# Feed-forward layers of a two-layer decoder step: eight block products per weight panel become seven

## What is computed

```python
def sq_relu_mlp(xn, w_up, w_down):
    h = jax.nn.relu(xn @ w_up)          # (tokens, 1024) @ (1024, 4096)
    return (h * h) @ w_down             # (tokens, 4096) @ (4096, 1024)

h = h + sq_relu_mlp(rmsnorm(h, g_mlp[l]), w_up[l], w_down[l])
```

## Time and profile before

| | |
|---|---|
| median of three runs | 1596.13 us |
| profiled execution, first to last instruction | 1593.0 us |
| feed-forward of layer 0 (32 panels) | about 378 to 788 us |
| feed-forward of layer 1 (32 panels) | about 1164 to 1587 us |
| busy share of TensorE / VectorE / ScalarE / GpSimd | 99 / 44 / 41 / 27 % |
| granted TensorE clock, mean | 0.999 |

### The profile page before, as it was taken

How to read it: one execution, slowest core, us unless ns; L and a number is a source line. 1 busy time by engine, 2 the same in 40 slices (tenths; PEclk the granted TensorE clock), 3 DMA queues, 4 the chain that set the end, 5 groups by cost and what they waited for, 6 DMA issues and landing times.

```text
span 1593.0 us, 34954 instructions
## 1 busy us (share of the span) xinstructions
PE 1575.9 (99%) x13744; PEld 1503.1 (94%) x13744; DVE 694.3 (44%) x1349; ACT 652.3 (41%) x996; POOL 434.9 (27%) x382
## 2 busy tenths in 40 slices
PE   8999999999999999999999999999999999999998
PEld 8999999989999999999998888887999999999998
DVE  8866666663212112112335888889532121121223
ACT  6544444433313213223334777678433132231333
POOL 3000000003443333434342211111433334344331
PEclk9999999999999999999999999999999999999999
DMA  6233332222222322222235554554222222222221
GB/s 190 54 100 83 82 82 84 91 88 80 81 82 77 106 79 79 79 79 79 79 97 190 203 178 146 160 174 134 72 65 92 91 79 80 79 79 79 79 80 60
DMA packets 169516, 158.11 MB, mean 99 GB/s; under 512 B 5388, under 2 KB 160084, under 8 KB 169428
## 3 DMA queue, kind: packets, MB, share of 16 engines
q1 hardware_dynamic: 151346, 147.34, 29.2%
q10 hardware_dynamic: 18082, 9.48, 2.1%
HBM read 145.00 MB, written 11.80 MB: 98 GB/s over the span
## 4 chain that ended last, share of the span: by engine, by line
PE 97%; DVE 1%; issue 1%; ACT 0%; DMA 0%; DVEq 0%; ACTq 0%
PE acc L2012 70%; PE acc L2359 6%; PE pM L2417 3%; PE acc L2272 1%; PE pL L2132 1%; PE pO L2431 1%; PE pL L2400 1%; PE acc L2474 1%; PE pO L2463 1%; PE acc L2491 1%; PE pM L2201 1%; PE acc L2463 1%; PE acc L2656 1%; PE pL L2183 1%; PE pL L2155 0%
## 5 line engine op out<-in xcount | busy, mean ns | idle before, releaser
L490 POOL TENSOR_TENSOR wlo<-wraw,whi 128x512 fp32r<-128x512 f32 x288 | 365.7, 1302 | 904.8 <-ACT whi L583 904.8
L2012 PE MATMUL acc<-xa_hi,whi 128*128 128x288 f32 x1568 | 344.4, 301 | 0.0
L2012 PE MATMUL acc<-xa_hi,wlo 128*128 128x288 f32 x1568 | 335.8, 296 | 0.0
L2012 PE MATMUL acc<-xa_lo,whi 128*128 128x288 f32 x1568 | 335.3, 295 | 0.0
L583 ACT ACTIVATE whi<-wraw 128x2048 fp32r<-128x2048 f32 x90 | 172.0, 1911 | 305.6 <-PE acc L2012 300.7
L2012 PE MATMUL acc<-xb_hi,whi 128*128 128x288 f32 x1200 | 257.9, 297 | 0.8 <-issue 0.8
L2012 PEld LDWEIGHTS acc<-xa_hi,whi 128*128 128x128 f32 x1568 | 250.8, 189 | 7.2 <-issue 4.6
L2012 PE MATMUL acc<-xb_hi,wlo 128*128 128x288 f32 x1200 | 257.0, 296 | 0.0
L2012 PE MATMUL acc<-xb_lo,whi 128*128 128x288 f32 x1200 | 256.9, 296 | 0.0
L2012 PEld LDWEIGHTS acc<-xa_hi,wlo 128*128 128x128 f32 x1568 | 252.3, 188 | 0.0
L2012 PEld LDWEIGHTS acc<-xa_lo,whi 128*128 128x128 f32 x1568 | 251.9, 188 | 0.0
(11 more groups left out here) (427 smaller groups left out, 2094.5 us busy)
## 6 DMA issues: line engine op xcount, KB each, us to landing
wraw<-in_w_up_dram SPq DMA_DIRECT2D x64, 512.0 KB, 4.6
wraw<-in_w_down_dram SPq DMA_DIRECT2D x64, 512.0 KB, 4.0
Kp<-in_cache_k_dram SPq DMA_DIRECT2D x32, 512.0 KB, 4.2
Vp<-in_cache_v_dram SPq DMA_DIRECT2D x32, 512.0 KB, 5.3
wraw<-in_w_in_a_dram SPq DMA_DIRECT2D x30, 512.0 KB, 5.6
wraw<-in_w_kv_dram SPq DMA_DIRECT2D x16, 512.0 KB, 4.3
St<-in_state_hgrn_dram ACTq DMA_DIRECT2D x8, 512.0 KB, 6.3
out_dram<-Sn ACTq DMA_DIRECT2D x8, 512.0 KB, 4.8
```

The source lines that it names most:

```text
L490: ins = pool.tensor_tensor(wlo[s][:, k:k + 2, :], wraw[s][:, k:k + 2, :], whi[s][:, k:k + 2, :].bitcast(F32), ALU.subtract)
L2012: last = pe.matmul(acc[a][:, hf, 0:HALF], w[s][:, k, a * P:(a + 1) * P], x[:, k, hf * HALF:(hf + 1) * HALF], start=(k == 0 and n == 0), st ...
```

## The change

Both feed-forwards are computed by Strassen's scheme, in Winograd's form. A panel is seen as a 2x2 matrix of blocks: even or odd k in depth, first or second output block of 128. The activations are seen as 2x2 as well: even or odd k, first or second token half. Instead of 8 block products there are 7, each of depth 4 x 128 into one PSUM bank. The kernel calls such a panel a quad and numbers them by `G`; r = G mod 8 is its place in a chunk, 0 to 3 up and 4 to 7 down. A quad is 7 x 4 x 3 = 84 matmuls. The last chunk's down projection of layer 1 stays as it was (`last_down`), so 60 of 64 panels change.

- Weights: VectorE makes four sums and differences of 512 columns a quad (`sum1` to `sum4`). The seven pieces are each split into high part by ScalarE (`piece_high`) and low part by GpSimd (`piece_low`), 512 columns each. There is one set of seven piece buffers for high and one for low; a piece is replaced when its product of the quad before is done.
- Activations: for each pair of k blocks VectorE makes four differences in three operations (`t_13`, `t_2`, `t_4`). ScalarE and VectorE split 7 instead of 4 half blocks (`pair_high`, `pair_low`); the operand tiles `X_*`, `H_*` hold seven slots of 288.
- Results: products that belong to several outputs share banks. A quad uses four banks, A to D, and A three times over. In an up quad ScalarE copies four banks to `H_f` (`copy_out`) and VectorE adds two more times 576 columns (`add_first`, `add_second`) ahead of relu. In a down quad VectorE adds six parts to `hT` (`h_part_1` to `h_part_6`).
- At the entry of each feed-forward (`enter_mlp`) and in the first down quad (`first_quad` on TensorE) the order is written out so that the last pair comes late.
- The sum of squares goes over a smaller ring of tiles (`nrm3`), and the quads are written out one by one, without `Fori`.

The core of the diff ("..." marks what is left out):

```diff
+        PAIR = [P, NB // 2, N_PC, HALF]
...
+        def quarters(s):
+            v = wraw[s][:].rearrange("p (k e) n -> p e k n", e=2)
+        def pieces(s):
+            a11, a12, a21, a22 = quarters(s)
+            return [a11, St1[:], a12, St2[:], a22, a11, a21]
...
+            def raw_panel(G):
...
+                    sp.wait_ge(piece_lo, N_PC * (G - 1))
...
+                    sp.dma_start(wraw[G % 2][:, ks, :], src).then_inc(raw_in[G % 2], 16)
...
+            def piece_low(G):
+                for i in range(N_PC):
+                    pool.wait_ge(piece_hi, N_PC * G + i + 1)
+                    pool.tensor_tensor(p_lo[i][:], pieces(G % 2)[i], p_hi[i][:].bitcast(F32), ALU.subtract).then_inc(piece_lo, 1)
...
+            def piece_high(G, i):
+                if i in (0, 2, 4):
+                    act.wait_ge(raw_in[G % 2], 32 * (G // 2 + 1))
+                else:
+                    act.wait_ge(sums, 4 * G + (1, 2, 4, 3)[i // 2 if i < 6 else 3])
+                if G in (0, N_Q0):
+                    act.wait_ge(unit_done, (U_MLP0, U_MLP1)[G // N_Q0] - (2 if i < 3 else 0))
+                else:
+                    act.wait_ge(product_done, N_PC * (G - 1) + i + 1)
+                act.activation(p_hi[i][:], pieces(G % 2)[i], ACT.Copy).then_inc(piece_hi, 1)
...
+            def up_quad(G, call=None):
+                n, c, i = place(G)
+                e, prior, more = made(n, c), i > 0, G + 1 < (N_Q0, N_Q0 + N_Q1)[n]
+                plain_last = n == 1 and c == FCH - 1
+                if call is not None:
+                    piece_high(G, 5)
+                piece_high(G, 6)
+                copy_out(G, "A", 0, 1)
+                if more:
+                    piece_high(G + 1, 0)
+                if prior:
+                    square_pair(G - 1)
+                copy_out(G, "C", 3, 2)
+                if more:
+                    piece_high(G + 1, 1)
+                    piece_high(G + 1, 2)
+                if prior and not plain_last:
+                    pair_high(e, i - 1, H_hi, H_f, 0)
+                if prior and plain_last:
+                    act.wait_ge(squared, square_count(n, c, i - 1) + 1)
+                    act.activation(H_hi[:, i - 1, 0:4, :], H_f[:, i - 1, 0:4, :], ACT.Copy).then_inc(hid_hi, 1)
+                copy_out(G, "A", 1, 4)
+                if more:
+                    piece_high(G + 1, 3)
+                if prior and not plain_last:
+                    pair_high(e, i - 1, H_hi, H_f, 1)
+                copy_out(G, "D", 2, 5)
+                if more:
+                    piece_high(G + 1, 4)
+                if call is not None:
+                    norm_rstd(call)
+                if more:
+                    piece_high(G + 1, 5)
+            def down_quad(G, blocks=None, nxt=None):
+                n, c, r = place(G)
...
-            def add_to_h(Ub):
-                with dve.Fori(0, 4) as i:
-                    for a in range(2):
-                        hv = hT[:, bass.ds(2 * i + a, 1), :].rearrange("p o (a b) -> p (o a) b", a=2)
-                        dve.wait_ge(unit_done, Ub + 2 * i + a + 1)
-                        dve.tensor_tensor(hv, hv, accv(a), ALU.add).then_inc(acc_free[a], 1)
...
-                def hidden(c):
-                    with dve.Fori(0, 4) as i:
-                        for a in range(2):
-                            n = Hb + NB * c + 2 * i + a
-                            hb = bass.ds(2 * i + a, 1)
-                            dve.wait_ge(unit_done, Ub + 16 * c + 2 * i + a + 1)
-                            dve.wait_ge(sqr_done, n + 1)
-                            dve.scalar_tensor_tensor(out=t2v(relu_t[a]), in0=accv(a), scalar=0.0, in1=t2v(rstd), op0=ALU.max,
-                                                     op1=ALU.mult).then_inc(acc_free[a], 1)
-                            lo_part(hid_lo_t[:, hb, :].rearrange("p a t -> p (a t)"),
-                                    hid_hi_t[:, hb, :].rearrange("p a t -> p (a t)"), sqr_t[a][:], hid_hi, n + 1)
...
+            def sum1(G):
+                a11, a12, a21, a22 = quarters(G % 2)
+                dve.wait_ge(raw_in[G % 2], 32 * (G // 2 + 1))
+                if G:
+                    dve.wait_ge(piece_lo, N_PC * (G - 1) + 2)
+                dve.tensor_tensor(St1[:], a21, a22, ALU.add).then_inc(sums, 1)
+            def sum2(G):
+                a11, a12, a21, a22 = quarters(G % 2)
+                dve.wait_ge(sums, 4 * G + 1)
+                if G:
+                    dve.wait_ge(piece_lo, N_PC * (G - 1) + 4)
+                dve.tensor_tensor(St2[:], St1[:], a11, ALU.subtract).then_inc(sums, 1)
+            def sum3(G):
+                a11, a12, a21, a22 = quarters(G % 2)
+                dve.tensor_tensor(a21, a11, a21, ALU.subtract).then_inc(sums, 1)
+            def sum4(G):
+                a11, a12, a21, a22 = quarters(G % 2)
+                dve.wait_ge(sums, 4 * G + 3)
+                dve.wait_ge(piece_lo, N_PC * G + 1)
+                dve.tensor_tensor(a11, a12, St2[:], ALU.subtract).then_inc(sums, 1)
+            def t_13(e, i, full, want):
+                dve.wait_ge(*want)
+                dve.tensor_tensor(full[:, i, 4:6, :], full[:, i, 1:4:2, :], full[:, i, 0:2, :], ALU.subtract).then_inc(t_made, 1)
+            def t_2(e, i, full):
+                dve.wait_ge(t_made, 12 * e + 3 * i + 1)
+                dve.tensor_tensor(full[:, i, 6, :], full[:, i, 3, :], full[:, i, 4, :], ALU.subtract).then_inc(t_made, 1)
+            def t_4(e, i, full):
+                dve.wait_ge(t_made, 12 * e + 3 * i + 2)
...
+            def operand_low(e, i, part, k, lo, hi, full):
+                dve.wait_ge(op_hi, XS * e + k)
+                dve.tensor_tensor(lo[:, i, part, :], full[:, i, part, :], hi[:, i, part, :].bitcast(F32), ALU.subtract
+                                  ).then_inc(op_lo, 1)
+            def pair_low(e, i, part, lo, hi, full):
+                operand_low(e, i, (slice(0, 4), slice(4, 7))[part], 2 * i + part + 1, lo, hi, full)
+            def add_first(G):
+                i, u = place(G)[2], up_count(G)
+                dve.wait_ge(copied, 4 * u + 3)
+                dve.wait_ge(product_done, N_PC * G + 6)
+                dve.tensor_tensor(both(H_f, i, 0), both(H_f, i, 0), bank_pair(G), ALU.add).then_inc(added, 1)
+            def add_second(G):
+                i, u = place(G)[2], up_count(G)
+                dve.wait_ge(copied, 4 * u + 4)
+                dve.wait_ge(product_done, N_PC * G + 7)
...
+            def relu_pair(G):
+                i, u = place(G)[2], up_count(G)
+                dve.wait_ge(added, 2 * u + 2)
+                v = H_f[:, i, 0:4, :].rearrange("p (b a) t -> p b (a t)", a=2)
+                dve.scalar_tensor_tensor(out=v, in0=v, scalar=0.0,
+                                         in1=rstd[:].rearrange("p (b t) -> p b t", b=1).to_broadcast([P, 2, T]), op0=ALU.max,
+                                         op1=ALU.mult).then_inc(relued, 1)
...
+            def up_quad(G):
+                n, c, i = place(G)
+                e, end = made(n, c), (N_Q0, N_Q0 + N_Q1)[n]
+                plain_last = n == 1 and c == FCH - 1
+                if i:
+                    add_second(G - 1)
+                    relu_pair(G - 1)
+                elif c:
+                    h_part_6(G - 1)
+                if G + 1 < end:
+                    sum2(G + 1)
+                if i and not plain_last:
+                    t_all(e, i - 1, H_f, (squared, square_count(n, c, i - 1) + 1))
+                if G + 1 < end:
+                    sum3(G + 1)
+                if i and not plain_last:
+                    pair_low(e, i - 1, 0, H_lo, H_hi, H_f)
+                if i and plain_last:
+                    hidden_low(2 * i - 2)
+                if G + 1 < end:
+                    sum4(G + 1)
+                if i and not plain_last:
+                    pair_low(e, i - 1, 1, H_lo, H_hi, H_f)
+                if i and plain_last:
+                    hidden_low(2 * i - 1)
+                add_first(G)
+                if i == 3:
+                    relu_block(G, 0)
+                if G + 2 < end:
+                    sum1(G + 2)
+            def h_add_part(G, b, t, which, k):
...
+            def first_down_quad(G):
+                n, c, r = place(G)
+                e, end = made(n, c), (N_Q0, N_Q0 + N_Q1)[n]
+                add_second(G - 1)
+                relu_block(G - 1, 1)
+                t_13(e, 3, H_f, (squared, square_count(n, c, 3) + 2))
+                last_low(e, 0, H_lo, H_hi, H_f)
+                t_2(e, 3, H_f)
+                t_4(e, 3, H_f)
+                last_low(e, 1, H_lo, H_hi, H_f)
+                last_low(e, 2, H_lo, H_hi, H_f)
+                h_part_1(G)
+                last_low(e, 3, H_lo, H_hi, H_f)
+                last_low(e, 4, H_lo, H_hi, H_f)
+                sum2(G + 1)
+                h_part_2(G)
+                sum3(G + 1)
+                h_part_3(G)
+                sum4(G + 1)
```

(94 more changed lines are left out.)

531 lines of the change are left out of this document (384 added, 147 removed).

## The result

The changed kernel takes 1659.63 us in the median of four runs (1658.24 to 1662.00); the kernel before took 1596.60 beside it (1595.74 to 1597.59). The ratio is 1.0395, with a 95% interval of 1.038 to 1.041. The forecast was 1612 us, slower by 1.0%, with a range of 1562 to 1668: the direction and the range held, but the kernel lost four times what was forecast. The profiled execution has a span of 1656.5 us, where the sum was made for 1608.6; 47.9 us have to be explained.

What follows compares the result with a forecast made beforehand. TensorE bounded the old kernel; VectorE and GpSimd taking turns would eat its 96 us gain. 1593.0 + 1.6 (turns) + 10 (ends) + 4 (late weights) = 1608.6, plus 3.1 from span to median: 1612 us, range 1562 to 1668.

Steps and rivals of the forecast that it cites:

- The turns: Heavy quads: VectorE operations with two SBUF inputs and GpSimd's exclude each other; one standing alone costs its duration less 0.25 us.
- Rival (1): Turns between VectorE and GpSimd cost nothing, since operations find gaps; TensorE stays the bound, 1510 us; chance 0.07.
- (2): GpSimd slips in behind every VectorE operation, so all get 0.25 us off: chunk 99.8, whole 1574 us; chance 0.20.
- Rival (4): No VectorE operation with two SBUF inputs overlaps GpSimd's: 114.8 us a chunk, 1700 us in all; chance 0.08.
- rival (3): VectorE stands before sum1 for weights, 3.1 us late, half of it in 31 quads: about 1658 us; chance 0.15.
- The sum over a chunk: Per full chunk, GpSimd 70.7 plus VectorE 44.1 minus 11.25 overlap: 103.5 us, against TensorE's 89.6 and 102.4 before.
- stays under that: Heavy quad: VectorE's chain add, relu, square, t, high part, bank copy, about 10 us with turns, stays under 15.2 us.
- The mechanism inside a heavy quad: Heavy quads take near 15 us, TensorE waiting for GpSimd's low pieces; waits for copied banks would mean VectorE's order bounds.
- Entries: Two feed-forward entries: piece 4's high part stands behind four operations on ScalarE; TensorE misses it by some 3 us each.
- Ends: Behind the first feed-forward and ahead of the last down projection: 2 us each; with entries +10, between 3 and 20.
- the 3 us of work ahead: 3 us taken off each feed-forward's sum for work done ahead, giving 769.6 us against 768.0: +1.6.
- the late weights: Raw weights' loads reach VectorE's sum1 some 0.2 us late in 21 heavy quads: +4 us.

## Why the prediction was right and wrong

**TensorE's side: right.** A light quad takes 11.19 us for 84 matmuls, 133.2 ns each, forecast 11.2.

**The turns: right, in size and place.** The means of GpSimd's and VectorE's operations came as forecast, and with GpSimd out of the way the chunk is 90.7. Rival (1), turns that cost nothing, is out, and so is (2), whose chunk was 99.8. Rival (4), with no overlap at all, had 114.8 a chunk; 107.1 were measured. (By its own terms rival (3) comes to 1656, not 1658.) The Trainium skill has the turns as an exclusive lock for a whole instruction ("SBUF — State Buffer", section "SBUF: two separate sides"); the runs agree that the other waits (0.15 us became 1.25). The quarter microsecond of overlap is that of the earlier trace rows; in the loop shown above the second difference ends 0.31 us after the GpSimd operation that it waited for, so about 0.14 of its 0.45 overlap.

**The sum over a chunk: too small by 3.6 us, seven times, 25 us.** This is the step that failed: one sum over the whole chunk, in place of the longer of chain and sum in each quad. Two terms of it were wrong. The sum let the pair of engines finish light quads in 10.6 us and carry the rest over; but TensorE needs 11.2 in each, and they took 4 x 11.19 = 44.8, not 42.4: +2.4. And r4, priced as the bare sum of 15.2, took 18.5 in the mean: there TensorE has nothing left to do but wait for relu, square, differences, high and low parts of the last pair, one behind the other with a turn at each. I had walked the queue for one heavy up quad and used the sum for the rest; the sentence that this chain "stays under that" was worked out for the up quads and is false for r4: +3.3. The three heavy up quads took 43.9 together, where three times 15.3 are 45.9: -2.0, which nearly makes good the first term. What is left of the 3.6 is mostly r4.

**The mechanism inside a heavy quad: half right.** I had TensorE waiting for GpSimd's pieces. It waits for bank copies, since the loop through VectorE and ScalarE (15.7) comes a little ahead of the pair's sum (15.2). That the sizes are nearly the same is luck, as the halved low parts show.

**Entries: 3 us each forecast, 11.2 measured, +16.4.** The step named ScalarE as what comes late. It was VectorE's queue: the last two blocks of h are added behind low parts of 1152 elements that take turns with GpSimd (4.51 us for two, of 1152 and 864, which take 1.36 and 1.05 alone), and later three small low parts take 4.78. In the kernel with seven products in the up panels alone, adding the seventh block earlier, with the last pair's low parts ahead of a sum, gained 4.5 to 4.9 in the entry quad; the two moves were not tried apart, and neither was the rest.

**Ends.** The first feed-forward's last chunk takes 111.8 us and 2.0 follow before the next projection's first matmul, so 6.7 above a steady chunk, where 2 were forecast: the low parts and squares for the next projection stand in VectorE's queue ahead of the additions that free a bank. The second's last four quads took 44.9, forecast 50.7: 5.8 less. They are like those of the run with seven products in the up panels alone, and again I had charged turns that lie in slack. Ahead of the last down projection TensorE stands for 7.0 us (6.8 of it is the "issue" above), where 2 were forecast: its first matmul starts at 1590.87, just as GpSimd ends the fourth low part of that panel, begun at 1583.99. And the 3 us of work ahead that I had taken off each feed-forward were not there (+6), nor the late weights (-4).

In sum: 25.2 + 16.4 + 4.7 + 5.0 - 5.8 + 6 - 4 = 47.5 of 47.9 us. The direction and the place inside the range came although the entries and r4, 40 us together, were not foreseen; that the range held them is luck, since its upper end was set beyond rival (3), late weights, which did not come.

## What to carry to other kernels

Where two engines take turns, work out both the sum of their durations and the longest chain through them, stage by stage: in one with slack turns cost nothing, and in one where the bound engine waits for the chain each step can cost a turn of the other engine (up to 1.1 us here), however short it is. Slack in a light stage isn't lent to the next one beyond what buffers hold, so sum stages by the larger of the engines' times, not over the whole. Before a scheme with fewer multiplications is given up, apply it only where its additions lie in slack: in the up panels alone it gains 2.0% here.

## What the runs showed of the hardware

An operation with two SBUF inputs on VectorE that comes while a GpSimd operation of 512 elements runs waits for the rest of that one, up to about 1.1 us, whatever its own length: 8 elements took 1.25 us instead of 0.15 (mean 0.41 to 0.67, since GpSimd wasn't always busy), 288 took 1.43 instead of 0.45, 512 up to 1.78 instead of 0.68, and the relu of 1152, which came 0.46 us before a GpSimd operation's end (525.87), 1.67 instead of 1.36. With GpSimd operations of half the length 288 elements took 0.87.

After waits of 1 to 3.5 us in heavy quads TensorE was granted 1.2 instead of 2.4 GHz in some of the matmuls behind them (0.94 over a chunk). The stretches of the earlier trace rows had it at full throughout.

A plain panel of 96 matmuls took 12.64 us in the unrolled variants, 131.7 ns a matmul, against 133.3 before. Why was not tried.
